# Four buffers of split weights, moved to four different places modulo 128 bytes

## What is computed

```python
# first block, per layer
z = rms_norm(h_res, attn_norm_g[l]) @ w_in[l]
...
h_res = h_res + jnp.concatenate([y_mla, y_ret], axis=-1) @ w_out[l]
gate, up = jnp.split(rms_norm(h_res, ffn_norm_g[l]) @ w_gate_up[l], 2, axis=-1)
h_res = h_res + (jax.nn.silu(gate) * up) @ w_down[l]
# second block, each of its feed-forward steps
g, u = jnp.split(h @ w_in, 2, axis=-1)
return (jax.nn.silu(g) * u) @ w_out
```

## Time and profile before

| | |
|---|---|
| median of 3 runs | 2441.07 us |
| lowest and highest | 2436.27 and 2443.59 us |
| span of the profiled execution (its own time outside the span is not given) | 2431.8 us |
| TensorE busy | 2286.2 us, 94% of the span |
| VectorE busy | 1481.2 us, 61% |
| ScalarE busy | 836.9 us, 34% |
| GpSimd busy | 178.6 us, 7% |
| DMA, mean | 141 GB/s |
| mean granted TensorE clock | 0.960 of 2.4 GHz |

### The profile page before, as it was taken

How to read it: one execution, slowest core, us unless ns; L and a number is a source line. 1 busy time by engine, 2 the same in 40 slices (tenths; PEclk the granted TensorE clock), 3 DMA queues, 4 the chain that set the end, 5 groups by cost and what they waited for, 6 DMA issues and landing times. The chain is left out here.

```text
span 2431.8 us, 36081 instructions
## 1 busy us (share of the span) xinstructions
PE 2286.2 (94%) x13542; PEld 2034.7 (84%) x13542; DVE 1481.2 (61%) x2237; ACT 836.9 (34%) x1137; POOL 178.6 (7%) x222
## 2 busy tenths in 40 slices
PE   7998999999999899999669999989999998989998
PEld 7888999988999788888558888878888887858998
DVE  4636776454777777588777867773333345375555
ACT  4424334333534432222232212232212233264443
POOL 0110000110000010000311000010000001100000
PEclk9989999998999999999779999999999999999999
DMA  5403675321565455555125555432222233212453
GB/s 197 148 35 135 208 236 184 119 100 41 196 226 205 163 196 179 168 190 177 48 100 194 179 175 182 163 131 87 91 99 96 75 106 104 87 36 103 170 194 121
DMA packets 66867, 343.12 MB, mean 141 GB/s; under 512 B 7264, under 2 KB 10592, under 8 KB 44000
## 3 DMA queue, kind: packets, MB, share of 16 engines
q1 hardware_dynamic: 46048, 266.50, 31.7%
q0 software_dynamic: 20736, 75.51, 9.8%
HBM read 340.93 MB, written 1.05 MB: 141 GB/s over the span
## 5 line engine op out<-in xcount | busy, mean ns | idle before, releaser
L644 PE MATMUL gpt<-xn_hi,w_hi 128*128 128x512 f32 (+2 forms) x2656 | 886.4, 334 | 31.4 <-DVE xn_lo L1931 25.0
L645 PE MATMUL gpt<-xn_lo,w_hi 128*128 128x512 f32 (+2 forms) x2656 | 881.5, 332 | 0.0
L646 PE MATMUL gpt<-xn_hi,w_lo 128*128 128x512 f32 (+2 forms) x2656 | 881.3, 332 | 0.0
L1402 DVE TENSOR_TENSOR w_lo<-raw,w_hi 128x2048 fp32r<-128x2048 f32 (+4 forms) x289 | 569.0, 1969 | 299.6 <-ACT w_hi L1045 298.2
L1045 ACT ACTIVATE w_hi<-raw 128x2048 fp32r<-128x2048 f32 (+4 forms) x292 | 481.8, 1651 | 399.9 <-PE gpt L646 354.4
L644 PEld LDWEIGHTS gpt<-xn_hi,w_hi 128*128 128x128 f32 x2656 | 506.1, 191 | 79.2 <-DVE xn_lo L1931 25.7
L645 PEld LDWEIGHTS gpt<-xn_lo,w_hi 128*128 128x128 f32 x2656 | 506.2, 191 | 45.5
L646 PEld LDWEIGHTS gpt<-xn_hi,w_lo 128*128 128x128 f32 x2656 | 506.1, 191 | 45.4
L644 PE MATMUL gpt<-mid_hi,w_hi 128*128 128x512 f32 (+2 forms) x1016 | 343.3, 338 | 2.5 <-DVE w_lo L1402 1.3
L646 PE MATMUL gpt<-mid_hi,w_lo 128*128 128x512 f32 (+2 forms) x1016 | 342.3, 337 | 0.0
L645 PE MATMUL gpt<-mid_lo,w_hi 128*128 128x512 f32 (+2 forms) x1016 | 342.3, 337 | 0.0
(11 more groups left out here) (277 smaller groups left out, 1859.9 us busy)
## 6 DMA issues: line engine op xcount, KB each, us to landing
raw<-in_up_a SPq DMA_DIRECT2D x72, 1024.0 KB, 4.9
ada_w<-in_ada POOLq DMA_DIRECT2D x144, 512.0 KB, 3.8
raw<-in_up_b SPq DMA_DIRECT2D x60, 1024.0 KB, 4.9
raw<-in_down_a SPq DMA_DIRECT2D x48, 768.0 KB, 4.2
raw<-in_down_b SPq DMA_DIRECT2D x48, 640.0 KB, 3.8
raw<-in_win SPq DMA_DIRECT2D x20, 1024.0 KB, 4.9
raw<-in_qkv SPq DMA_DIRECT2D x12, 1024.0 KB, 4.9
raw<-in_wout SPq DMA_DIRECT2D x8, 1024.0 KB, 5.3
```

What stands on the lines that cost most here:

```text
L644: mm(o, w_hi[b][:, j, :], hi(k), start=(k == 0), stop=False)
L645: mm(o, w_hi[b][:, j, :], lo(k), start=False, stop=False)
L646: last = mm(o, w_lo[b][:, j, :], hi(k), start=False, stop=(k == kt - 1))
L1402: V.tensor_tensor(w_lo[b][:, 0:tiles, :], raw[b][:, 0:tiles, :], w_hi[b][:, 0:tiles, :].bitcast(F32), ALU.subtract).then_inc(lo_ready, 1)
```

## The change

Between the four buffers of split weights stand gaps of 32 bytes, and the order becomes `w_hi0`, `w_lo0`, `w_hi1`, `w_lo1` with a gap behind each:

```diff
-        w_hi = [sb(f"w_hi{b}", [P, SIDE_T, P], F32R) for b in range(2)]
-        w_lo = [sb(f"w_lo{b}", [P, SIDE_T, P], F32R) for b in range(2)]
+        w_hi = [None, None]
+        w_lo = [None, None]
+        for b in range(2):
+            w_hi[b] = sb(f"w_hi{b}", [P, SIDE_T, P], F32R)
+            sb(f"w_gap{b}", [P, 8])
+            w_lo[b] = sb(f"w_lo{b}", [P, SIDE_T, P], F32R)
+            sb(f"w_gap{b + 2}", [P, 8])
```

## The result

| | before | after |
|---|---|---|
| median of 9 runs each | 2440.64 us | 2450.55 us |
| lowest and highest | 2436.27 and 2445.89 | 2442.96 and 2466.72 |
| ratio, 95% interval | | 1.0044 (1.0025 to 1.0063) |
| profiled execution, its time | not given | 2444.82 us |
| its span | 2431.8 us | 2443.1 us |

A forecast was written before the change was run, and what follows sets the result against it. The prediction took TensorE's matmul count times pitch as the bound. Terms of +17.0, -2.3, -2.9, -1.8 and +0.4 us sum to +10.4, on 2441.1 giving 2451.5 us, range 2419 to 2475.

The forecast's parts named there:

- The bound: Streaming stages: TensorE has no gap, so time is the number of matmuls times their pitch.
- The mechanism: Matmuls: pitch changes with the distance between weights and moving operand, 7.4 ns between `xn` and `mid` at 512 columns.
- The modulus: Address distances were counted modulo 128 bytes: 0 in all loads on `xn` before, 96 on `mid`.
- two stay at 0: On `xn`, two of six weight loads keep distance 0 and four leave it: +17.0 us at 512 columns.
- The price "as 96": Any distance other than 0 costs what 96 does: 7.4 ns more at 512 columns, 1.4 less at 256, 2.1 at 272.
- The average over the six loads: Each term took the share of six weight loads changing distance: four of six on `xn`, one of six on `mid`.
- The test that I had named: `xn` pitch at 512 columns rises from 226.8 to about 231.7 ns, slots of b = 1 slower than b = 0.
- The other parts: `mid` at 512 columns gains 1.8 us, one of six loads coming to 0; splits, waits and slot loads stand as before.
- That the weights' place does not matter: Rival: the moving operand's own begin at 32 sets the pitch, nothing moves, 2441 us; chance 0.27.
- That the spread frees the stream: Rival: buffers at different places dephase TensorE's reads and weight loads, 18.6 us gained, 2422.5 us; chance 0.20.
- The much slower case: Rival: weights beginning at 32 or 96 cost separately, every 512-column matmul 7.4 ns more, 36.4 us lost, 2477.5; chance 0.13.
- The 215.8 ns: 512 columns at 2.4 GHz plus 2.5 ns, the skill's rule for a warm stream, set against the trace's 226.8 ns.

The follow-up runs named there:

- run 1: Against the kernel before: all four weight buffers moved to 32 modulo 128 by gaps of 32 and 96 bytes; ratio 1.0062.
- run 9: Against the kernel before: only the weights moved, all four by 64 bytes, all else at its place modulo 256; ratio 1.0034.
- run 6: The change with 128 more bytes behind `ada_w`, giving distances 0, 32, 64, 96 on `xn`; ratio 1.0083 to the kernel before.
- run 7: Against the kernel before: only `w_lo0` and `w_lo1` moved, by 32 bytes, `w_hi` staying at distance 0 from `xn`; ratio 1.0099.
- run 2: Against the kernel before: all four weight buffers at 64 modulo 128 by gaps of 16 floats on both sides; ratio 1.0021.
- run 8: Against the kernel before: `mid` at the weights' place by a 96-byte gap, and columns 8 to 263 for 256 tokens in feed-forward passes; ratio 0.9929.
- run 3: Against the kernel before: a gap of 96 bytes ahead of `mid_hi` puts `mid_hi` and `mid_lo` at the weights' place; ratio 0.9960.
- run 10: Against the kernel before: all four weight buffers 16 bytes further, everything else at its place modulo 256; ratio 1.0073.

## Why the prediction was right, and where it was wrong

**The bound** was right: TensorE in the streaming stages, without a gap; what was lost is busy time of TensorE, and nothing of it a wait.

**The mechanism** was right. The difference between `xn` and `mid` in the rows of before was a matter of distance between weights and moving operand, and not of the moving operand's own place: run 1 moved the short pitch from one to the other, and run 9 took it away from `xn` by changing the weights' place only.

**The modulus** was wrong, and with it the step "two stay at 0". I reckoned modulo 128, where the 128 bytes by which everything else moves on are nothing. Modulo 256 they are half a turn, and no load on `xn` stays at 0. That would have made +25.6 us for `xn` at 512 columns by my own price, not +17.0. It measured +19.1, since the pitch became 232.3 ns and not 234.2. So one error added to the term what the other took away, and that the sum of 10.4 us came as near the measured 10.7 as it did is luck; the ledger by pitches, 13.1 us, is the fairer comparison.

**The price "as 96"** for every distance other than 0 held roughly at 512 columns for 16, 32, 64, 112, 128, 160 and 224 (232.8 to 233.4 ns where all weights lie alike, 6.1 to 6.7 above distance 0 and not 7.4) and failed at 192 (228.9). At 256 and 272 columns it did not hold: 256 columns took from 115.9 ns (distance 64) to 120.0 (0, 112 and 160), so that `xn` at 256 columns gave back 5.0 us and not 2.3; 272 columns on `xn` gave nothing instead of 2.9 us.

**The average over the six loads** was wrong. Runs 6 and 7 show that one load in three at another distance loses the short pitch on average of all three. The test that I had named, slots of b = 1 slower than those of b = 0, went the other way: 233.4 ns for b = 0 and 231.2 for b = 1 in the 480 matmuls from 1020.60 us on. Modulo 256 the loads of `w_hi1` are those at 192, the mild distance, but that this is the reason is not shown: run 6 has nearly the same two values, 233.2 and 231.3, with `w_hi` at 0 and 64, and 64 alone is not mild (run 9). What makes b = 1 the better mixture stays open.

**The other parts** held: `mid` at 512 columns moved by -2.6 us (-1.8 forecast), though not by the load that comes to distance 0, as I had it: in the stage from 953.66 us on, the slots of b = 0, which have it, are at 233.2 ns and those of b = 1 at 231.6. The splits changed by 1 ns, TensorE's wait for `w_lo` from 8.7 to 8.6 us.

**The rivals.** That the weights' place does not matter is refuted by run 9. That the spread frees the stream is refuted at 512 columns. At 256 columns on `xn` the change did gain 2 ns for each matmul (117.8), but run 2, with all weights at one place, has the same 117.8 and run 9, again with one place, 115.9: the distance gives it, and no spread is needed. The short pitches everywhere, its price of 18.6 us, are to be had by the opposite of a spread: run 8, with all at one place for 512 columns, gains 17.3. The much slower case, an odd begin of the weights as such, is refuted by run 1, where weights and `mid` both lie at 32 modulo 128 (160 modulo 256) and take the short pitch. That two read streams of TensorE have no influence on each other, as the separate ports in the Trainium skill, SBUF — State Buffer, section Who interferes with whom, would let one expect, does not hold here: in run 9 the moving operand kept its place modulo 256, and each matmul of 512 columns on `xn` took 6.6 ns more by the place of its weights alone. The 215.8 ns that the prediction sets beside its 226.8 are, in the section it names (the Trainium skill, TensorE: Matmul & The Clock Gate, section Back-to-back issue gap), the gap of an isolated matmul; for a stream with a weight load for each matmul that section gives about 131 ns at 512 columns. No run here shows either: the shortest pitch at 512 columns is 226.7 ns.

## What to carry to other kernels

Where TensorE streams float32r matmuls with a weight load each, try both operands' buffers at the same place modulo 256 bytes for 512 columns, which was best in this kernel, and look at the sum of small tensors between them: here a few odd sizes left `mid` at distance 96, and a gap of 96 bytes gained 10 us (run 3). For shorter rows another distance can be better, and a column offset gives it without moving a buffer. Read it off as begin-to-begin distances of neighbouring matmuls; the mean duration of a group shows it less exactly (at 512 columns on `xn` 391 to 393 ns before, 395 to 398 after). A change of any allocation can shift it unseen, so a comparison of two kernels should first compare these distances.

## What the runs showed of the hardware

- At full clock, a matmul's pitch depends on the distance of its operands' addresses, with a period of no more than 256 bytes: 226.7 ns at 0 against 233.2 at 16 (run 10) for 512 columns.
- At half clock no such dependence was seen for 272 columns: on `xn` 226.7 ns at distance 0 (the kernel before, mean of 107), 226.7 at 64 (run 9, 75) and 226.8 with the mixed places of the change (79); on `cn` 227 ns at distance 160 and with the mixed places.
- The other engines' writes to and reads of the same memory have no part in it that could be seen: with DVE busy 75 of 100 us, as in the first window of the earlier trace rows, the pitch is the same as with 31 of 100, in this window of the kernel before (443 matmuls in both):

```profile
1840.00:1940.00 100.00, 100.00 (x443) 82.80 (x442) 31.43 (x27) 25.62 (x27) 0.00 (x0) 1.00 0.26 90
```

  Nor is the longer pitch theirs: in run 9, at distance 64, the pitches on `xn` at 512 columns have a mean of 233.3 ns where VectorE and ScalarE are both idle (791 of them), 233.4 where VectorE alone is busy (1433) and 233.3 where both are (266).

What in the reads of weights and moving operand meets, and why 512 columns prefer 0 and 256 columns 64, was not tested and stays open.
